# A decoder step on one core: key product at a pair's end, remainders and splits moved forward, another engine waits for y

## The reference

```
q = (c_q @ w_q_up)                       # 512 -> 16 heads x (64 + 32 rotary)
kv = (c_kv @ w_kv_up)                    # prompt: keys k_nope and values v, 64 each per head
s = (q_nope . k_nope + q_pe . k_pe) * scale, causal;  p = softmax(s);  o = p @ v
# sampled group: q_lat = q_nope . w_uk, scores against 16 cached pages of 128 latent rows
# per sequence and its own new rows; o_lat = p @ latent rows; o = o_lat @ w_uv
outputs: y_prompt, y_sample, the new latent rows (prompt_ckv, sample_ckv), rotary keys
         (prompt_kpe, sample_kpe), S5 end states
y = rmsnorm(x)                           # at the very end, over 1024 channels
```

## Time and profile before

| | us |
|---|---|
| runs, median (lowest to highest) | 1617.96 (1614.13 to 1618.27) |
| the profiled execution's own time | 1621.41 |
| its span, first to last instruction | 1619.8 |
| PE busy in the span | 1515.4 (94%) |
| DVE, ACT, POOL busy | 771.9, 603.9, 366.7 |
| mean granted TensorE clock | 0.962 of full |

### The profile page before, as it was taken

How to read it: one execution, slowest core, us unless ns; L and a number is a source line. 1 busy time by engine, 2 the same in 40 slices (tenths; PEclk the granted TensorE clock), 3 DMA queues, 4 the chain that set the end, 5 groups by cost and what they waited for, 6 DMA issues and landing times.

```text
span 1619.8 us, 32125 instructions
## 1 busy us (share of the span) xinstructions
PE 1515.4 (94%) x11453; PEld 1425.9 (88%) x11453; DVE 771.9 (48%) x1227; ACT 603.9 (37%) x1085; POOL 366.7 (23%) x430
## 2 busy tenths in 40 slices
PE   5989988889999899999999999789999999999995
PEld 5966666668988899999999999689999999999994
DVE  3866546545554454343244454964443522344332
ACT  6344454475654233321133233342333311233221
POOL 0286665434421102210022133020012200122000
PEclk9989899889999999999999999899999999999997
DMA  7123323323323222222222465512222222222211
GB/s 175 24 60 83 85 83 88 104 87 112 95 86 121 63 81 78 87 82 79 81 86 78 137 187 160 199 31 81 78 79 80 82 88 87 79 78 83 83 57 59
DMA packets 245279, 147.57 MB, mean 91 GB/s; under 512 B 42071, under 2 KB 239614, under 8 KB 244190
## 3 DMA queue, kind: packets, MB, share of 16 engines
q1 hardware_dynamic: 238114, 139.39, 29.4%
q0 software_dynamic: 6704, 7.20, 1.7%
q10 hardware_dynamic: 396, 0.13, 0.0%
HBM read 128.42 MB, written 18.26 MB: 91 GB/s over the span
## 4 chain that ended last, share of the span: by engine, by line
PE 86%; DVE 6%; ACT 3%; issue 2%; DMA 1%; POOL 1%; SPq 0%; ACTq 0%; DVEq 0%; POOLq 0%
PE bank L861 60%; PE bank L781 7%; PE bank L1103 3%; PE bank L976 3%; PE bank L1068 3%; PE bank L924 3%; PE bank L941 2%; PE bank L990 1%; PE bank L984 1%; ACT arena L1358 1%; DVE tmpa L2315 1%; DVE arena L2020 1%; DVE arena L2342 1%; DVE sq L2315 1%; PE bank L1009 1%
## 5 line engine op out<-in xcount | busy, mean ns | idle before, releaser
L861 PE MATMUL bank<-arena_parts,wR 128*128 128x288 f32 x4224 | 567.1, 296 | 6.0 <-ACT arena_parts L1435 3.7
L861 PEld LDWEIGHTS bank<-arena_parts,wR 128*128 128x128 f32 x4224 | 563.2, 188 | 7.8 <-issue 5.9
L861 PE MATMUL bank<-side_parts,wR 128*128 128x288 f32 x3360 | 447.3, 295 | 1.1 <-DVE tmpa L2387 1.1
L861 PEld LDWEIGHTS bank<-side_parts,wR 128*128 128x128 f32 x3360 | 445.5, 188 | 1.5 <-issue 1.3
L1841 DVE TENSOR_TENSOR wR<-wraw,wR 128x1024 fp32r<-128x1024 f32 x159 | 232.8, 1464 | 238.1 <-ACT wR L1421 236.6
L744 POOL TENSOR_TENSOR arena_parts<-sq,arena_parts 128x576 f32 x64 | 91.7, 1433 | 674.4 <-ACT arena_parts L1654 674.4
L1421 ACT ACTIVATE wR<-wraw 128x1024 fp32r<-128x1024 f32 x159 | 167.2, 1052 | 201.9 <-PE bank L861 187.4
L1358 ACT ACTIVATE arena<-bank 128x256 f32<-128x256 f32 (+9 forms) x223 | 96.1, 446 | 151.7 <-PE bank L984 53.0
L1651 ACT ACTIVATE tmpa<-bank 128x576 f32<-128x576 f32 x64 | 41.8, 653 | 195.3 <-PE bank L861 195.3
L2238 DVE TENSOR_TENSOR sq<-tmpa 128x576 f32<-128x576 f32 x64 | 48.5, 758 | 127.0 <-ACT tmpa L1651 127.0
L781 PE MATMUL bank<-ident,arena 128*128 128x128 f32 (+4 forms) x400 | 70.7, 299 | 20.0 <-DVE arena L2020 15.9
(11 more groups left out here) (301 smaller groups left out, 1622.3 us busy)
## 6 DMA issues: line engine op xcount, KB each, us to landing
wraw<-in_mlp_w SPq DMA_DIRECT2D x128, 512.0 KB, 3.9
side<-in_cache_ckv SPq DMA_DIRECT2D x128, 128.0 KB, 2.1
wraw<-in_ssm_w_glu SPq DMA_DIRECT2D x16, 512.0 KB, 3.9
s_state_to_out<-side SPq DMA_DIRECT2D x16, 256.0 KB, 2.5
s_in_to_state<-yblk SPq DMA_DIRECT2D x8, 512.0 KB, 2.6
s_in_to_out<-side SPq DMA_DIRECT2D x64, 64.0 KB
wraw<-in_mla_w_o SPq DMA_DIRECT2D x8, 512.0 KB, 4.5
side<-s_in_to_state SPq DMA_DIRECT2D x2, 2048.0 KB, 13.0
```

What stands on the lines that cost most here:

```text
L861: return pe.matmul(bank[:, a, 0:HALF], wR[:, s, wp, k, :], tokens(k, xp)[:, a * HALF:(a + 1) * HALF], start=(first and j == 0), stop=(last ...
```

## The change

Seven edits, and two more at the end of y.

1. The key product of pair p+1 (`keys_product`) is issued at unit 6 of pair p, into bank6; only pair 0 has it at its old place. The loop is written as pair 0, a loop over six pairs, and pair 7 without it. The key-weight transposes go to bank45 instead of bank6.
2. Unit 0's scores wait for head 0's queries and keys alone; unit 1's for head 1's.
3. `cut_queries_of(0)` stands after block 4's rows on ACT, and POOL's remainders for pair 0 come before the S5 products, once block 5 is done.
4. In decode's start the splits of sequence 0 come first, then the samples' rows, the first two groups of pages, then the prompt's rows, then the first output-weight block, on PE, ACT and DVE alike. The prompt's rows go through bank45 alone.
5. POOL waits once for all nine row copies before it writes the rows out.
6. The token sums are two sets: `acc` without tile 7's square, issued right after the last product, and tile 7's square itself, accumulated in bank23. DVE's last `add_square` is gone. ACT copies tile 7's transposes before it takes the root.
7. ACT issues the transfers of token blocks 2 and 3 of y itself, SP those of 0, 1 and the samples; SP waits for all of them, POOL no more.

```diff
@@ sync
-            for j in (0, 2, 1, 3, 4):
-                if j in (2, 3):
-                    sp.wait_ge(fin_ya, j - 1)
-                else:
-                    sp.wait_ge(fin_y, {0: 1, 1: 2, 4: 3}[j])
+            for j in (0, 1, BLK):
+                sp.wait_ge(fin_y, {0: 1, 1: 2, BLK: 3}[j])
...
+            sp.wait_ge(y_out, 16 * (BLK + 1))
@@ gpsimd
+            pool.wait_ge(blk_done, 6)
+            rest_of_weights(0)
             pool.wait_ge(pw_sb, 1)
...
-            pool.wait_ge(y_out, 16 * (BLK + 1))
@@ tensor
+            def keys_product(p):
+                pe.wait_ge(hw_in, p * 96 + 96)
+                for r in range(2):
+                    ins = pe.matmul(bank6[:, :], wkv[:, r, 0, :, :].rearrange("p h n -> p (h n)"), ckvT[:, r, 0:SEQ],
+                                    start=(r == 0), stop=(r == 1))
+                ins.then_inc(k_done, 1)
...
+                pe.wait_ge(qn_sb, p * 2 + 1)
+                pe.wait_ge(qr_sb, p * 2 + 1)
+                pe.wait_ge(k_sb, p * 2 + 1)
+                pe.wait_ge(kpe_raw, 1)
+                unit_scores(p, 0)
                 pe.wait_ge(qn_sb, p * 2 + 2)
                 pe.wait_ge(qr_sb, p * 2 + 2)
                 pe.wait_ge(k_sb, p * 2 + 2)
-                pe.wait_ge(kpe_raw, 1)
-                unit_scores(p, 0)
                 unit_scores(p, 1)
...
+                    if u == 6 and not last:
+                        keys_product(p + 1)
...
+            turn_pages(0, 0, 0)
+            pe.wait_ge(nat_sb, 4)
+            turn_pages(0, 0, 1)
+            for j in range(BLK + 1):
+                if j >= 2:
+                    pe.wait_ge(nat_sb, 4 + j - 1)
...
             mlp(1)
+            pe.wait_ge(sq_used, Q_END - 1)
+            pe.wait_ge(tile_free, T_OUT - 1)
+            token_sums(acc, True, False)
             tokens_down(KT - 1)
-            pe.wait_ge(sq_used, Q_END)
+            pe.wait_ge(sq_ready, Q_END)
+            token_sums(sq[:, 1, :], False, True).then_inc(ss_done, 1)
@@ scalar
+                if m == 4:
+                    cut_queries_of(0)
...
-            cut_queries_of(0)
             root(1)
...
             cut_queries(0, 0)
-            cut_block(B_B)
+            for j, src in enumerate((bank45[:, 0, :], bank45[:, 1, :], bank6[:, :], bank7[:, :])):
...
             pages_turned(0, 0, 0)
             pages_turned(0, 0, 1)
+            for j in range(BLK):
...
+            cut_block(B_B)
             phase((0, 0), None, (1, 1))
...
             mlp(1)
+            tokens_down(KT - 1)
             act.wait_ge(var_ready, 4)
...
-            tokens_down(KT - 1)
...
+            for j in (2, 3):
+                act.wait_ge(fin_ya, j - 1)
+                act.dma_start(O["y_prompt"][0, j * P:(j + 1) * P, :], ynat[:, j, :]).then_inc(y_out, 16)
```

More of the change, by code:

```diff
@@ L626, in _, with rest_of_weights @@
             pool.memset(bbD[:, :, :, :], 0.0).then_inc(bbD_sb, 1)
+            def rest_of_weights(p):
+                pool.wait_ge(wq_hi, p + 1)
+                if not isinstance(p, int):
+                    apart(pool)
+                for h in range(2):
+                    for to, at, n in ((0, 0, HD), (96, 80, 16), (112, 64, 16)):
+                        pool.tensor_tensor(wqL[:, :, h, to:to + n], wq_raw[h][:, :, at:at + n],
+                                           wqH[:, :, h, to:to + n].bitcast(F32), ALU.subtract).then_inc(wq_lo, 1)
+            pool.wait_ge(blk_done, 6)
+            rest_of_weights(0)
             pool.wait_ge(pw_sb, 1)
@@ L646, in _, with chunk_of_pair @@
             pool.wait_ge(tab_in, 16)
[L647 to L654 removed]
+            pool.wait_ge(blk_done, B_B)
+            def chunk_of_pair(p):
+                if not isinstance(p, int):
+                    rest_of_weights(p)
                 def chunk_product(n, out, b_re, b_im):
@@ L980, in _ @@
                 pe.wait_ge(var_ready, 2)
+                if isinstance(p, int) and p == 0:
+                    keys_product(p)
                 pe.wait_ge(o_sb, p * 2 + CREDIT)
-                for r in range(2):
-                    ins = pe.matmul(bank45[:, 0, :], wkv[:, r, 0, :, :].rearrange("p h n -> p (h n)"), ckvT[:, r, 0:SEQ],
-                                    start=(r == 0), stop=(r == 1))
-                ins.then_inc(k_done, 1)
                 pe.wait_ge(yt_sb, p + CREDIT)
@@ L2258, in down @@
                             residual_scaled(it * 2 + j, (t0 + j) % 2, it * 2 + (16 * i + 8 * half + j))
-                            if half == 1:
+                            if half == 1 and not (isinstance(it, int) and i == 1 and it * 2 + j == KT - 1):
                                 add_square(it * 2 + (q0 + j), j)
```

76 lines of the change are left out of this document (35 added, 41 removed).

## The result

The changed kernel takes 1605.19 us (median of nine runs, 1599.29 to 1611.79), the kernel before 1617.96 (nine runs, 1614.13 to 1623.11). The ratio is 0.9914, 95% interval 0.9892 to 0.9936: 10 to 17 us faster, the medians 12.8 apart. The forecast was 1602.0 in a range of 1594 to 1608.5. The profiled executions stand at 1605.46 and 1621.41 us. Their spans are 16.2 us apart, 3.4 more than the medians, since the profiled execution of the kernel before stood 3.4 above its median.

A forecast was written before the change was run, and what follows sets the result against it. PE, on the chain most of the time, was taken as the bound through its waits and half-clock work. Terms 6.0 + 0.1 + 2.2 + 1.2 + 6.5 = 16.0, with the clock 18.9, gave 1602 us, range 1594 to 1608.5.

The forecast's parts named there:

- The wait for y: Kernel's end: SP waits instead of POOL, so 7.8 us after the last byte become about 1.3; 6.5 us gained.
- The drain stays: Rival: SP, or POOL once the others are in, needs 6 us at the end; 1608 us, chance 0.07.
- The end before the transfers: End of y: earlier sums and ACT's copies off the path bring scaling and first transfer forward; 1.2 us gained.
- Decode's start: Last pair's copy to third page group: less ACT work and waiting, minus handshakes; 2.2 us gained, bounds 0.5 and 3.3.
- handshakes: Decode's start: prompt's rows alternate between bank45's halves, PE transposing, ACT copying; up to 0.5 us waiting at three.
- The pair: Pair loop: moved key product and split score waits gain 0.8 us net per pair, 6.0 in sum (0 to 9).
- The split wait: Pair loop: new PE idle time of 0.7 us between units 0 and 1's scores speaks for a clock fall in each pair.
- The clock term: Pair loop: one half-clock stretch fewer than seven; 2.9 us gained, bounds -6 and +12.
- the clock takes some back: Rival: all eight pairs have the half-clock stretch, pair 0 a longer one; 1608 us, chance 0.12.
- Pair 0 and the remainders: Pair 0: POOL's remainders moved ahead of the S5 products gain 0.1 us net, bounds -2 and +5.15.

The follow-up runs named there:

- the kernel with `fill(4)`: The changed kernel plus four PE products that nobody reads (bf16, 128x512) in each pair, between the scores of units 0 and 1: 1589.24 us, ratio 0.9813.

## Where the prediction was right and where wrong

- **The wait for y: right in place and size.** 6.5 forecast, 6.9 in the trace, 6.8 when done alone. SP's drain was put at 0.36 us from the earlier trace rows, where it ran during the transfers; behind them it takes 0.007. "The drain stays" is out.
- **The end before the transfers: right in place, too small.** 1.2 forecast, 2.1 measured. ACT's copies left the path as said (0.7). The second set of sums starts 1.46 us after DVE's last addition, where the sums started 2.23 after it, and ten like matmuls take 1.55 us where eight and two took 2.16: 1.4 together, where the forecast had 0.5. It had put the start 0.2 too late and left the sums as long as they were.
- **Decode's start: the mis-sized term.** 2.2 forecast with a bound of 3.3, and a third page group at 10 to 11 us after the copy; it comes at 8.8, and this part of the kernel gained 6.4. Two steps failed: the count of what leaves ACT's way, and the half clock that was left in place. Between the copy and the third group ACT was idle for 2.7 us before and is for 0.5 now: 2.2 instead of 1.6. The samples' four copies take 0.50 us each instead of 0.61 (0.4), and DVE's cut of the weight block (1.2), which stood ahead of the first page's remainder, had held it for 0.4. The 0.4 that I charged for handshakes didn't come. With the 1.04 of the block that is 4.0 of the 4.2 measured. The other 2.2 us come between the third group and the first product of probabilities, and are the clock: the stretch to 346.6 has no counterpart, though PE did nothing but transposes from 325.7 to 335.0, with waits of up to 2.2 us (1.00 in the window from 325.6, above). The Trainium skill's rule of TensorE: Matmul & The Clock Gate, "Part 4: PE-mode transpose", that transposes don't count as busy, was said to agree with the earlier trace rows. This window does not bear it out, and the measurement decides; the added transposes speak against it too, as far as one trace does.
- **The pair: the mechanism right, the value wiped out.** At full clock a pair gained 0.96 us (0.8 forecast), key products and unit 6 stand as foreseen, and latent queries start 0.55 us after DVE's last step, as said (185.26 to 185.81). But pairs with half clock take 30.5 to 31.2, not 29.8. That is the wrong number: I had priced a stretch at 2.9 us from the old pairs and let its length stand, when it went from 6.8 to 10.2. The prediction named what goes with it, that the densest part leaves the weak stretch, and used it only as an argument against a better clock. The split wait, which it expected to push the clock down, did not lengthen the stretches (the run without it has 10.2 too).
- **The clock term, 2.9: right in number, wrong in sign.** One stretch fewer came, as I took it (five and pair 0's instead of seven), and they are longer: 68 us of half clock in the pair loop against 51 before. What fell away was decode's stretch, which I had left in place. The rival "the clock takes some back" (0.12) describes the pairs best; its sum of 1608 was not reached because of decode and the end.
- **Pair 0 and the remainders: 0.1 forecast, -0.6 measured.** It lies within the bounds. POOL's remainders and DVE held each other up as feared (5.41 instead of 3.06 us; DVE's addition at 69.43 took 1.55, the like one at 73.76 took 0.88), and the half clock came earlier and lasted 17.1 us.
- **The 2.7 us lost later** have no term. No instruction moved there. DVE's cuts of the weight blocks come about 10 us sooner all the way from 556 to 998 us of the kernel before and about 7.2 sooner from 1127 on, so it is lost around S5, where the half clock fell on other work (a stretch from 1050.3 to 1057.1 has no counterpart).

The total came out near by luck, because the errors cancelled: against the sum of 18.9 decode, the end and the wait brought 5.5 more, and the pairs (4.1 instead of 8.9), pair 0 and the later stretch 8.2 less. That makes the 16.2 of the spans. Still open: what exactly makes the clock fall. Without added products it falls 11.5 to 12.1 us into a pair where the key product has left, and 14.7 to 15.0 into one where it has not. The latent queries end 11.5 and 12.5 us into such pairs, so the thin work lies ahead of the fall both times. With products or transposes put there the clock mostly stays up. Whether they do it by their work or by giving all pairs one length isn't separated by these runs; it held at two lengths, 27.4 and 28.6 us. Why the stretches are longer without the key product is open as well.

## What to carry to other kernels

An edit that takes dense work out of a part of PE's that has waits can lengthen the half-clock stretch and lose most of its gain. Look at how long the stretches are, not only at how many, and time the edit once more with products that nobody reads in PE's waits. Seven small products a pair brought more on top of the change (16.9 us, from 1603.8 to 1586.9, with edit 3 undone in both) than the whole change (12.8), and only 6.8 in the kernel before. Give the last wait of a program to an engine whose drain is short, and let the one with a long drain finish early.

## What was not expected of the hardware

- POOL's drain takes 6.7 us with nothing of its own under way (at the end of the kernel before). In the changed kernel it takes 7.9, begun at 1486.8 while POOL's last product runs to 1487.9, so again 6.8 behind it. ACT's takes 2.17 us beside its scaling of 2.19 in the kernel with the wait alone moved, and 0.15 when that is over. SP's takes 0.36 during its transfers and 7 ns behind them.
- The same code runs its seven pairs in 207.5 us in one kernel's execution and in 213.2 in another's, and the old code in 211.6 and 205.9: the code is the same, the stretches differ.
- PE held the full clock through 9.3 us of transposes alone, and lost it in pairs in which it was busy for 93% (28.84 of 31.10 us, the time at half clock included).
- One addition of DVE (0.75 us) beside one of POOL (1.43) takes 1.41 and 1.93 us when they meet, and in the kernel with `fill(4)` they meet in each of pairs 2 to 7 (DVE's addition takes 1.38 to 1.49 there).
